# Two diffusion blocks on one core: GpSimd writes the inversion's level-3 masks ahead of the rates, and a feed forward's last side turn goes behind the first down tile

## The reference

```python
def wkv_scan(S0, r, w, k, v, kk, b, reverse):
    def step(S, inp):
        r_t, w_t, k_t, v_t, kk_t, b_t = inp
        sa = -jnp.einsum('bhij,bhj->bhi', S, kk_t)
        S = S * w_t[:, :, None, :] + sa[..., :, None] * b_t[:, :, None, :] + v_t[..., :, None] * k_t[:, :, None, :]
        return S, jnp.einsum('bhij,bhj->bhi', S, r_t)
    xs = tuple(jnp.swapaxes(t, 0, 1) for t in (r, w, k, v, kk, b))
    S, ys = lax.scan(step, S0, xs, reverse=reverse)
    return S, jnp.swapaxes(ys, 0, 1)
```

```python
    h = h + g2 * swiglu(modulate(h, norm2_g[l], sh2, sc2), ffn_w_in[l], ffn_w_out[l])
def swiglu(h, w_in, w_out):
    g, u = jnp.split(h @ w_in, 2, axis=-1)
    return (jax.nn.silu(g) * u) @ w_out
mod = silu_c @ ada_w[l] + ada_b[l]
```

## Time and profile before

| | |
|---|---|
| median of 3 runs | 4181.57 us (4180.88 to 4189.18) |
| profiled execution, time | 4176.3 us |
| its span, first to last instruction | 4174.5 us |
| mean granted TensorE clock | 0.936 |
| PE busy | 3883.7 us (93%) |
| PEld busy | 3225.2 us (77%) |
| DVE busy | 1338.2 us (32%) |
| ACT busy | 1250.4 us (30%) |
| POOL busy | 1249.9 us (30%) |
| DMA | 343.50 MB, 82 GB/s over the span |

### The profile page before, as it was taken

One profiled execution on the slowest core, in us unless ns is written; L12 is line 12 of the kernel. 1 busy time (PEld: TensorE's weight loads), 2 busy tenths in 40 slices (PEclk: granted clock), 3 DMA queues, 4 the chain that ended last, 5 costly groups with the idle time before them and its releaser, 6 DMA issues. The chain is left out here.

```text
span 4174.5 us, 77349 instructions
## 1 busy us (share of the span) xinstructions
PE 3883.7 (93%) x32782; PEld 3225.2 (77%) x32782; DVE 1338.2 (32%) x2687; ACT 1250.4 (30%) x2182; POOL 1249.9 (30%) x658
## 2 busy tenths in 40 slices
PE   6988999999989999979699999889999989999997
PEld 5867788888777777768598888768888868667785
DVE  3344211111453211165555665351111040443111
ACT  3234311121355322232233343231112132543222
POOL 1201222222334343332222233122222223544442
PEclk8999999999999999989778888999999989999998
DMA  4232232332200435222201100123232211012221
GB/s 170 67 113 90 93 113 86 116 106 71 72 9 31 179 118 183 104 101 106 77 23 26 25 23 23 60 83 120 84 112 104 79 56 62 29 43 82 96 87 69
DMA packets 119705, 343.50 MB, mean 82 GB/s; under 512 B 34559, under 2 KB 41087, under 8 KB 119039
## 3 DMA queue, kind: packets, MB, share of 16 engines
q1 hardware_dynamic: 119423, 339.41, 23.5%
HBM read 324.55 MB, written 16.93 MB: 82 GB/s over the span
## 5 line engine op out<-in xcount | busy, mean ns | idle before, releaser
L204 POOL TENSOR_TENSOR feed_low<-ring,feed_high 128x1024 fp32r<-128x1024 f32 (+1 forms) x236 | 620.4, 2629 | 1372.9 <-ACT feed_high L197 1341.0
L221 PE MATMUL ps<-hn_high,feed_high 128*128 128x512 f32 x2016 | 720.3, 357 | 9.3 <-DVE h L1182 5.1
L221 PE MATMUL ps<-hn_low,feed_high 128*128 128x512 f32 x2016 | 714.2, 354 | 0.0
L221 PE MATMUL ps<-hn_high,feed_low 128*128 128x512 f32 x2016 | 713.3, 354 | 0.0
L221 PEld LDWEIGHTS ps<-hn_high,feed_high 128*128 128x128 f32 x2016 | 381.2, 189 | 90.0 <-issue 24.6
L221 PEld LDWEIGHTS ps<-hn_high,feed_low 128*128 128x128 f32 x2016 | 381.0, 189 | 53.6
L221 PEld LDWEIGHTS ps<-hn_low,feed_high 128*128 128x128 f32 x2016 | 381.3, 189 | 51.5
L1357 DVE TENSOR_TENSOR ps<-feed_gate,ps 128x768 f32<-128x768 f32 (+1 forms) x88 | 73.0, 830 | 1004.4 <-PE ps L221 985.6
L197 ACT ACTIVATE feed_high<-ring 128x1024 fp32r<-128x1024 f32 (+1 forms) x240 | 272.7, 1138 | 380.8 <-PE ps L221 380.8
L221 PE MATMUL ps<-feed_hid_high,feed_high 128*128 128x512 f32 (+1 forms) x1056 | 381.3, 361 | 0.0
L221 PE MATMUL ps<-feed_hid_high,feed_low 128*128 128x512 f32 (+1 forms) x1056 | 378.8, 359 | 0.0
(11 more groups left out here) (578 smaller groups left out, 7576.7 us busy)
## 6 DMA issues: line engine op xcount, KB each, us to landing
feed_side_ring<-in_ada SPq DMA_DIRECT2D x144, 512.0 KB, 5.8
ring<-in_ffn_g SPq DMA_DIRECT2D x88, 512.0 KB, 3.5
ring<-in_ffn_u SPq DMA_DIRECT2D x88, 512.0 KB, 3.5
ring<-in_ffn_d SPq DMA_DIRECT2D x64, 704.0 KB, 4.1
diff_side_ring<-in_ada SPq DMA_DIRECT2D x32, 512.0 KB, 4.2
ring<-in_od_in SPq DMA_DIRECT2D x24, 512.0 KB, 3.5
ring<-in_ev_in SPq DMA_DIRECT2D x23, 512.0 KB, 4.6
ring<-in_even_in SPq DMA_DIRECT2D x20, 512.0 KB, 3.5
```

The lines of the kernel that those rows point to most:

```text
L204: pool.tensor_tensor(self.low[:, j % self.slots, 0:w], feed.ring[:, slot, 0:w], self.high[:, j % self.slots, 0:w].bitcast(F32), ALU.subtra ...
L221: mm = pe.matmul(dst, weights[a], values[b], start=first and n == 0, stop=last and n == 2)
```

## The change

On POOL, `advance` writes the four masks of level 3 ahead of `rates(j, 0)`, and the four of level 4 directly behind these and ahead of `add_bonus(e)`. In the feed forward, the turn of a half's last side group goes from ahead of the first down tile to behind it. No instruction is added or taken away.

```diff
--- before.py
+++ after.py
@@ -1275,8 +1275,6 @@
                     for p in range(2):
                         chunk(i, p, 2 * i + (p + 1))
                 feed.at = down
-                if next_c:
-                    sm.turn(pe, 6 * h + 5)
                 pe.wait_ge(hid_low_ready, HALF * (h + 1) - 1)
                 pe.wait_ge(y_free, 8 * h + 1)
                 slot = split.wait(pe, 0, 0)
@@ -1287,6 +1285,8 @@
                         mm = split.products_of(pe, GATE[:, a:b], (split.high[:, slot, c * P:(c + 1) * P], split.low[:, slot, c * P:(c + 1) * P]),
                                                (hid[0][:, c, a:b], hid[1][:, c, a:b]), c == 0, c == HALF - 1)
                 mm.then_inc(split.products, 1)
+                if next_c:
+                    sm.turn(pe, 6 * h + 5)
                 for n in range(1, DOWN):
                     pe.wait_ge(y_free, 8 * h + n + 1)
                     tile_products(k, pe, n // 4, n % 4, region(k, n % 2, tokens), hid, tokens, split, chunks=range(HALF))
@@ -2755,16 +2755,15 @@
                         level_mask(i, 1, c).then_inc(S["ct_ready"], 1)
                     for c in range(4):
                         level_mask(i, 2, c).then_inc(S["ct_ready"], 1)
+                    for c in range(4):
+                        level_mask(i, 3, c).then_inc(S["ct_ready"], 1)
                 if preparing:
                     rates(j, 0)
                 if inverting:
                     for c in range(4):
-                        level_mask(i, 3, c).then_inc(S["ct_ready"], 1)
+                        level_mask(i, 4, c).then_inc(S["ct_ready"], 1)
                 if reading:
                     add_bonus(e)
-                if inverting:
-                    for c in range(4):
-                        level_mask(i, 4, c).then_inc(S["ct_ready"], 1)
                 if preparing:
                     rates(j, 1)
```

## The result

| | before | after |
|---|---|---|
| median | 4183.52 us (4180.88 to 4189.18, 4 runs) | 4121.69 us (4120.41 to 4122.66, 4 runs) |
| profiled execution, time | 4176.3 us | 4122.66 us |
| its span | 4174.5 us | 4120.9 us |
| mean granted clock | 0.936 | 0.946 |

The ratio is 0.9858, 95% interval 0.9845 to 0.9871: faster, by 1.4%. The forecast was 4112 us, the range 4094 to 4142. From profile to profile the gain is 53.6 us, where the sum had said 66.9; from median to median it is 61.8.

What follows compares the result with a forecast made beforehand. PE, busy 93% of the span, was taken as the bound, so gains come from its idle time and clock. 41.8 + 8.3 + 11.7 + 5.1 = 66.9 us off 4176.3 gives 4109.4, adjusted to 4112; range 4094 to 4142.

Steps and rivals of the forecast that it cites:

- its first step: At G3, PE idles 3.0 us because POOL writes rates before level 3's masks; the clock then is 0.50 for 36 us.
- Pairs 2 to 5: Level 3's masks no longer wait for the rates, the clock holds to level 4: 10.4 us a pair, 41.8 for four.
- DVE's loss beside the masks: Scan and centre running beside POOL's level-3 masks lose 0.8 us, the centre alone slowed; bounds nothing and 2.6.
- signs named for "right": No POOL wait over 0.5 us, clock 1.00 from G3 to U4, scan near 1.78, about 92 us from pair to pair.
- Rival B: Scan doubles too, DVE loses 2.6 us, U2 waits 2.3, the clock falls in all four pairs: 4148; chance 0.11.
- The last pair: Level 4's masks ahead of the bonus remove G4's wait: recurrence 7.5 us earlier, first step 0.8 more, 8.3 in all.
- The first pair: Loses its clock earlier, in level 1, waiting for DVE's first inverses; counted 0, up to 11 us if no fall.
- The feed forward's waits: First down tile replaces the turn's wait: 11.7 us for six halves, plus 5.1 of clock behind three of them.
- A: Clock still falls in some pairs, at U2 or in level 3; with two of four, 4126 or 4129; chance 0.18.
- C: Slower: masks beside scan and centre hold up ACT's copies longer than G3 was held; 4186 at 12 us loss; chance 0.02.
- D: No effect: G3 waits for something else at once, the down tile for its weights; 4176 stays; chance 0.03.
- The bound after: DVE at level 4 becomes the bound; PE idle for most of 2213.5 to 2218.5, the clock expected to fall there.

Runs made afterwards that it cites:

- ACT's copies first: Changed kernel with level 4's inverses before the second scan and four dense products in the first pair, plus G2's last copies before ACT's wait for the centre: 4102.14 us.
- small filler: Kernel before, plus 28 thrown-away products of 128 columns with zero weights between U2 and G3 of pairs two to five: 4176.23 us, ratio 0.9995.
- the dense one: Kernel before, plus ten thrown-away products of 512 columns with real weights between U2 and G3 of pairs two to five: 4176.84 us, ratio 1.0.

## Why the prediction was right

**The mechanism**, its first step, held: POOL's place in the order was the stall at G3, and the clock behind it was the larger price. Level 3's masks alone give 8.4 us in each of pairs 2 to 5 (55.3 to 46.85), though the wait was 3.0. A filler over the same wait gives at most 2 us a pair. So early masks are enough, and a busy PE over the old wait is not: behind both kinds of filler G3 still had waits of its own (0.58 us, or 0.49 and 0.78), and the clock fell there.

**The terms.**
- Pairs 2 to 5: 9.2 us each (36.9 in all), taken at 10.4. Three small shortfalls of the working make it (0.3, 0.7 and 0.35 us, less 0.2 elsewhere), each measured from the pair's first G1. U2's second half starts 18.95 us behind it, I had 18.65 (idle time 0.75, taken at 0.5). `updates` are 0.7 longer, because the bonus on POOL now falls beside them: 1.61 us for the product at L3231, where the earlier trace rows had 0.92. I had called the bonus hidden and had not asked what it slows. And level 4 from its first inverse to `lora_rate` takes 5.6 us, taken at 5.25. So `lora_rate` starts at 39.1, I had 37.95, and before 48.4.
- DVE's loss beside the masks: 1.26 us (0.69 on the scan, 0.57 on the centre), taken at 0.8, on the centre alone. Of the signs named for "right" this one failed, and the others came. The step that the scan keeps its 1.78 because it "already goes at the receptance's slowed pace" was wrong. The Trainium skill, GPSIMD Engine Reference, section Specifications, says that GpSimd contends with VectorE's instructions that have two SBUF inputs; the trace now agrees for the scan too, with 2.47 against 1.78. Not every overlap has a price: in the kernel before, the product of `query` (L3225) started at 2201.94 with POOL's first mask at 2201.97, and took its 0.92 us. Rival B's price, a doubling, was too high: the loss is half of its 2.6.
- The last pair: 6.4 us, taken at 8.3. Two things were missing. I had counted 3.7 us from the end of U4 to the recurrence, with two joins of 0.5 in it. It is 4.8: the 96 records of `join_second` alone take 1.66, and the two products that clear the output bank 1.0. And the clock falls once more just as the recurrence begins, so its first step gains nothing: 0.8.
- The first pair: 0, as measured (54.7, 54.9).
- The feed forward's waits, 11.7, and the clock behind them, 5.1: both came at their places. From the last side group of a half (L259) to ACT's work 20 to 30 us later, the changed kernel gains 3.8 us in three of the six halves (waits of 2.2, and 1.7 of clock), 2.2 in one and 1.5 in two: 16.6 of the 16.8 taken.
- What the sum had left out: 5.2 of these 16.6 are lost again outside the halves, so that 11.4 remain. The changed kernel is 1.1 us late already at the first of the six places, where it has run nothing that was changed; 1.2 go between the second half and the third, where the longer fall at L1607 lies, 1.4 between the fourth half and the first pair, 1.5 behind the sixth. What makes them is open. Part is the difference of any two executions. Whether PE's lead makes the falls longer is not shown: the run with the turn alone measured 12.1, and its interval (8 to 17.5 us) would hold 11.7 and 16.8.

That the feed forward's two parts leave 11.4 us, close to the waits alone, is chance, and so is a part of how near 4112 came to 4121.7: by the ratio the gain is 59 us, from profile to profile 54, and the two halves apart give 52.

Together the parts measured are 36.9, 6.4 and 11.4, less 1.1 between the pairs and in the first: 53.6.

**The rivals.** A (the clock falls in some pairs) did not come: it holds in all of pairs 2 to 5, over an idle time of 0.75 us before U2. The Trainium skill, TensorE: Matmul & The Clock Gate, section A second HAM failure mode, warns of frequent short idle times. The runs agree where the idle times were 0.49 and 0.78 in one G3 behind a filler. The 0.75 before U2 stood alone, and says nothing against it. But one idle time of 0.52 stood alone as well, in the first pair of the run with ACT's copies first, and the clock fell behind it; there small products stood ahead of it, and the gate's four products of 512 columns ahead of the 0.75. And behind one wait of 1.70 us, the same in all profiles, it fell in four of fourteen. Length alone does not decide, then; what does, no run here settles. B needed a loss of 2.6. C and D have nothing for them.

**The bound after.** I had said that DVE at level 4 would be the next bound and the clock would fall there. Both are in the trace (1.48 and 1.42 us before `join_first`, 0.50 behind them), and undoing it gives 14 us in the pairs, where 12 were expected.

## What to carry over

Where one engine's stall is followed by a long stretch at half the clock, look at what the waiting engine does just behind the stall: the price was 8.4 us for a wait of 3.0. Cost each instruction that is moved on GpSimd also by what it then runs beside on VectorE, and do so for what stands behind it in the list as well. A filler on TensorE was no substitute for the operand being early: over the wait at G3 it gave at most 2 us a pair and nothing that the whole time shows, and ahead of the recurrence it gave no gain either. And before a term of the account is called missing, look at its own place in the trace: the clock's 5.1 us were there, and were lost elsewhere.

## What the runs showed of the hardware

- GpSimd beside VectorE, here f32 on 128 partitions: scan of 780 elements 2.47 us instead of 1.78, a difference of 780 elements 1.54 instead of 0.97, a product of 768 elements 1.61 or 1.90 instead of 0.92; four masks 6.07 instead of 3.89.
- The inversion's products of 64 by 64 by 32 keep the clock at 1.00 once it is there, and did not bring it back: 0.50 in a window where PE is busy for 8.00 of 8.00 us.
- Filling the wait before G3 moved the clock's fall and did not stop it: it was at about 2203.5 in the second pair of before, 22.5 us behind the first G1; about 2 us later with the small filler (1.00 up to 2205, 0.99 to 2208, 0.50 from there) and about 5 with the dense one (1.00 up to 2210, 0.50 from 2212). Zero weights made no difference to the time.
- One wait of 1.70 us, in level 1 of the last pair and the same in all 14 profiles, left the clock at 1.00 in ten and was followed by a fall in four. One profile does not tell whether such a fall belongs to the kernel.
